# Shared read-outs and kept keys, and three sums of squares moved to ScalarE, in a hybrid attention, SSD and mLSTM block

## The chip, the cores and the metric

The kernel runs on one core of one Trainium2 chip. The metric is the device time of one execution, in microseconds (us), and lower is better. The engines are named as in the profile: PE (TensorE matmul) with PEld (its weight load), DVE (VectorE), ACT (ScalarE), POOL (GpSimd) and SP (the queue that issues most DMAs).

## The reference

Two token sequences (256 and 1024 tokens, width 1024) run through the same two layers, all in float32. Cut to what matters here:

```python
h = rmsnorm(x); [aq ak av | sz sxbc sdt | mq mk mv mo mi mf] = h @ W_in
x = x + concat(attention, bidirectional_ssd, bidirectional_mlstm) @ W_out
x = x + expert_choice_swiglu_moe(rmsnorm(x))

# mLSTM, per head (4 heads of 64), in chunks of 128, forward and backward
c_loc = einsum('bhcs,bcshe,bcshd->bched', w, vc, kc)     # state of a chunk: weighted keys times values
wq    = exp(dmat - m_l) * (q @ k.T)                      # inside the chunk, masked
num   = wq @ v + einsum(q, c_prev, sc)                   # + read-out of the state before the chunk
den   = max(|sum(wq) + einsum(q, n_prev, sc)|, exp(-m_l))
h     = rmsnorm(h_f + h_b) per head; y = sigmoid(o) * h
# SSD, per chunk: y = (cb * exp(segsum)) @ xdt + C @ prev * exp(a_cs)
# attention: q = rmsnorm(aq), k = rmsnorm(ak), per head
```

## The kernel before

Both sequences stand side by side as T = 1280 tokens, that is NC = 10 chunks of P = 128. Each engine has its own instruction stream, written out by hand, that runs in order and waits on semaphores. `link` makes an engine wait for its own last result before its next instruction. Float32 matmuls show two records each in the profile (transposes one). A layer has these stages, in this order of time:

- The input projection is cut into "units". A unit is 8 matmuls that accumulate over the model width (16 records); between units PE does the small products of the mixers, so that the mixers run in the shade of the projection. ACT copies each unit out of PSUM (`evac`).
- **SSD loop**, 10 chunks. Per chunk PE does 3 units, `ssd_products` and `ssd_sum`. The latter ends with four matmuls of 64 rows and 256 columns (two directions by two groups) that read the state before the chunk, `PREV`.
- **State loop of the mLSTM**, 8 steps (`STEPS`; the forward and the backward scan take one chunk each per step). PE: `turn_keys(n+1)` (4 transposes of the keys of two chunks into PSUM), one unit, and the state product. DVE: `weigh_keys(n+1)` multiplies the turned keys by their weights (from PSUM) and then updates the state. ACT only copies the unit out.
- **mLSTM loop**, 10 chunks, which is where most of the change lies. SP loads a row table for chunk c into one of two buffers `DMM[c % 2]` (`m_load`, which waits until chunk c-2 has been summed by PE, `nd_made`). The streams, in their own order, are, for c = 0 to 9:
  - PE: unit c, `ml_products(c+1)`, `ml_sum(c)`. The latter has 8 matmuls of 65 columns from `DMM` and `V`, and then 8 of 64 rows and 65 columns with the states `PREVM`. It waits for `ml_weights(c)` and for `ml_read(c-1)`.
  - POOL: `ml_mask(c+1, 0)`, `ml_mask(c+1, 1)` (L713); from c = 1, wait for `h_summed` of chunk c-1 and take the reciprocal root of its four sums (`rroot`, L643 and L644); for c = 2, 4, 6, 8 `attn_root` (the same on the six sums of q and k of an attention chunk); for c = 3, 5 `attn_norm` (L724, L728).
  - ACT: `ml_exp(c+1, 0)` (4 exponentials of 128 columns, L1001, after mask (c+1, 0)), wait for `ml_gate(c-2)`, `Tanh` of the output gate (L1010), `evac` of unit c (L890), `ml_exp(c+1, 1)`.
  - DVE: `ml_read(c-1)` (two operations of 520 columns out of PSUM), `ml_gate(c-2)` (after the root), `ml_output(c-1)` (the last three operations of which are the sum of the two directions, its square and the sum of squares per head, L1427), `attn_product` (q and k squared, odd c) or `attn_sum` (L1441, even c, from 2), and `ml_weights(c+1)` (two operations, after the exponentials).
- Output projection with the attention between its parts, then the experts, which are half of the span and are not touched.

Of the kernel before, what the change touches and what calls it, by code (L numbers as in the profile page):

```python
# [8 lines left out]
P = 128  # L9
NC = T // P  # L10
NP = SEQS[0] // P
KD = D // P
HD = 64
# [66 lines left out]
def has_next(i):  # L80
    return i not in (NP - 1, NC - 1)


STEPS = [i for i in range(NC) if has_next(i)]


# [42 lines left out]
def program(nc, wi, wo, wga, wup, wdn, par, cst, onehot, xp, xs_in, yp, ys, btab, h2p, h2s, flip):  # L129
# [4 lines left out]
    with ctx:  # L134
# [43 lines left out]
        UROW = VO[0:4, 0:2 * T].rearrange("p (d t) -> p d t", d=2)  # L178
        MROW = VO[0:4, 2 * T:4 * T].rearrange("p (d t) -> p d t", d=2)
        PREVM = MID[:, pv_at:pv_at + 2 * NC * 130].rearrange("p (d c h e) -> p d c h e", d=2, c=NC, h=2)  # L180
        QT = HT[:, 6144:6144 + 2 * T].rearrange("p (j t) -> p j t", j=2)
# [38 lines left out]
        JUNK = HT[:, 5 * D:6 * D]  # L220
        SQ = TMP[:, 1104:1488]

        AFF = [TMP[:, 0:512], SCR[:, 3584:4096]]
# [78 lines left out]
        layer_cleared = sem("layer_cleared")  # L302
        table_stored = sem("table_stored")
        bias_loaded = sem("bias_loaded")
# [7 lines left out]
        def layer_sem(name):  # L312
# [35 lines left out]
        mrow_stored = layer_sem("mrow_stored")  # L348
        cs_loaded = [layer_sem(f"cs_loaded{j}") for j in range(2)]
        m_loaded = [layer_sem(f"m_loaded{j}") for j in range(2)]  # L350
        d_shifted = layer_sem("d_shifted")
# [71 lines left out]
        w_made = layer_sem("w_made")  # L423
        kt_turned = layer_sem("kt_turned")
        mstate_made = layer_sem("mstate_made")
        wk_made = layer_sem("wk_made")
# [21 lines left out]
        quad_spread = layer_sem("quad_spread")  # L448
        kept_sems = [cst_loaded, hot_loaded, layer_done, layer_cleared, table_stored, bias_loaded, *x_loaded, *gathered, *quad_gathered, scattered_p,
                     scattered_s]  # L450
# [40 lines left out]
        with nc.Block(no_gpsimd_drain=True) as block:  # L491
            @block.sync
            def _(sp):
                for layer in range(DEPTH):
# [75 lines left out]
                    def cs_load(c):  # L570
                        if c >= 2:
                            sp.wait_ge(y_made, c - 1)
                        sp.dma_start(DM[:, c % 2],
                                     bass.AP(tensor=csr.tensor, offset=c * 24 * P, ap=[[0, P], [12 * P, 2], [1, 8 * P]])).then_inc(cs_loaded[c % 2], 16)

                    def m_load(c):
                        if c >= 2:
                            sp.wait_ge(nd_made, c - 1)
                        sp.dma_start(DMM[:, c % 2].rearrange("p d h t -> p (d h t)"),
                                     bass.AP(tensor=mrr.tensor, offset=c * 8 * P, ap=[[0, P], [1, 8 * P]])).then_inc(m_loaded[c % 2], 16)  # L580

                    sp.wait_ge(csrow_stored, 16)
                    sp.wait_ge(state_made, len(STEPS))
                    for c in range(NC):
                        cs_load(c)
                        if layer == 0 and c == 1:
                            sp.wait_ge(state_kept, len(STEPS))
                            sp.dma_start(btab[:, 0:NREL], table).then_inc(table_stored, 16)
                        if layer == 0 and c == 4:
                            sp.wait_ge(table_stored, 16)  # L590
# [45 lines left out]
            def _(pool):  # L636
                for layer in range(DEPTH):
# [34 lines left out]
                    def ssd_mask(c, d):  # L672
                        if d == 0:
                            pool.wait_ge(cs_loaded[c % 2], 16 * (c // 2 + 1))
# [33 lines left out]
                    def ml_mask(c, d):  # L708
                        if d == 0:
                            pool.wait_ge(m_loaded[c % 2], 16 * (c // 2 + 1))  # L710
# [132 lines left out]
            def _(act):  # L843
                for layer in range(DEPTH):
# [148 lines left out]
                    evac(U_ATT - 1)  # L993

                    for i in range(NC):
                        evac(U_ATT + i)
                    def ml_exp(c, d):
                        act.wait_ge(md_masked, 2 * c + d + 1)
                        for h in range(MH):
                            v = DMM[:, c % 2, d, h, :]  # L1000
                            link(act.activation(v, v, ACT.Exp, bias=U[:, c, d, h:h + 1], scale=-1.0), md_exp if h == MH - 1 else act_chain)  # L1001

                    ml_exp(0, 0)
                    ml_exp(0, 1)
                    for c in range(NC):
# [6 lines left out]
                        if c + 1 < NC:  # L1012
                            ml_exp(c + 1, 1)

                    def attn_exps(n, h0=0, h1=AH):
# [146 lines left out]
            def _(dve):  # L1162
                for layer in range(DEPTH):
# [212 lines left out]
                    def weigh_keys(n):  # L1376
                        dve.wait_ge(kt_turned, n + 1)
                        if n >= 2:
                            dve.wait_ge(mstate_made, n - 1)
                        for d in range(2):  # L1380
                            c = scan_chunk(d, STEPS[n])
                            tt(heads(WK[n % 2][:, 256 * d:256 * d + 256], 4), heads(ps[:, 4 + 2 * (n % 2), 256 * d:256 * d + 256], 4),
                               wide(WM[:, c, d, :], HD), ALU.mult, wk_made)
# [21 lines left out]
                    nd = TMP[:, 0:520]  # L1405
                    hsd = SCR[:, 3392:3904]
                    hs, hd = hsd[:, 0:256], hsd[:, 256:512]
# [10 lines left out]
                    def ml_output(c):  # L1418
# [4 lines left out]
                        link(dve.reciprocal(rec, den))  # L1423
                        tt(heads(hsd, 8), heads(nd, 8)[:, :, 0:HD], wide(rec, HD), ALU.mult)
                        tt(hs, hs, hd, ALU.add)
                        tt(hd, hs, hs, ALU.mult)
# [61 lines left out]
                    for c in range(NC):  # L1488
# [7 lines left out]
                        if c >= 1:  # L1496
                            ml_output(c - 1)
                        if 1 <= c <= 8:
                            if c % 2:
                                attn_product(c // 2)  # L1500
                            else:
                                attn_sum(c // 2 - 1)
                        if c + 1 < NC:
# [216 lines left out]
            def _(pe):  # L1720
                for layer in range(DEPTH):
# [177 lines left out]
                    def ssd_sum(c):  # L1899
# [26 lines left out]

                    def turn_keys(n):
                        if n >= 2:
                            pe.wait_ge(wk_made, 2 * (n - 1))
                        for d in range(2):  # L1930
                            c = scan_chunk(d, STEPS[n])
                            for q in range(2):
                                last = pe.transpose(ps[:, 4 + 2 * (n % 2), 256 * d + q * P:256 * d + (q + 1) * P],  # L1933
                                                    QK[:, 2 + q, c * P:(c + 1) * P], ident)
                        last.then_inc(kt_turned, 1)
# [33 lines left out]
                    def ml_sum(c):  # L1969
# [6 lines left out]
                        for j in range(2):  # L1976
                            for d in range(2):
# [468 lines left out]
```

## Time and profile before

| | |
|---|---|
| median of 3 runs | 2414.69 us (2413.03 to 2416.08) |
| profiled execution | 2412.42 us, span 2411.0 us |
| granted TensorE clock, mean | 0.991 |
| PE busy | 2336.8 us, 97% of the span |
| DVE busy | 1046.9 us, 43% |
| ACT busy | 585.4 us, 24% |
| POOL busy | 538.1 us, 22% |

The busy times are those of one profiled execution, in which the span runs from the first instruction to the last; 1.4 us of that execution lie around it. PE's busy time is modelled at its ends and hides short waits, so the starts of its instructions say more than its share.

### The profile page before, as it was taken

Reading aid. Unit: us, or ns where it says so; the run is one execution under the profiler, and the core shown is the slowest. Engines: PE = TensorE matmul, PEld = TensorE weight load, DVE = VectorE, ACT = ScalarE, POOL = GpSimd, SP = SyncE. Lnnn points to the kernel's source line nnn. Section 1 sums busy time; section 2 is a strip of 40 time slices with the busy share of each in tenths; the row PEclk is TensorE's granted clock in tenths of the full one; section 3 lists DMA queues with packets and bytes.
Section 4 is the critical chain, followed back from the end, with each engine's and each line's share of the span. In section 5 each row is a group of like instructions: output and inputs, shape, how many; then the busy total and the mean of one; then the engine's idle time right before and its main releaser. Section 6 shows DMA issues by size and latency. Waiting matters only on the chain.

```text
span 2411.0 us, 34301 instructions
## 1 busy us (share of the span) xinstructions
PE 2336.8 (97%) x13630; PEld 1683.5 (70%) x13630; DVE 1046.9 (43%) x1961; ACT 585.4 (24%) x1265; POOL 538.1 (22%) x550
## 2 busy tenths in 40 slices
PE   7999999999999999999889999999999999999998
PEld 4577578874555788877645775788745468888786
DVE  4851566596645111111148515665965451111111
ACT  3220232344332111111132202323443321111111
POOL 1011453144211111111110114531442111111111
PEclk9999999999999999999999999999999999999999
DMA  3102222121227988778331012221212279887783
GB/s 131 38 18 70 71 90 81 62 97 53 79 76 268 327 289 280 265 262 287 92 121 38 18 65 76 80 78 62 97 54 79 79 270 329 286 281 258 269 287 79
DMA packets 149344, 352.24 MB, mean 146 GB/s; under 512 B 9885, under 2 KB 38049, under 8 KB 149186
## 3 DMA queue, kind: packets, MB, share of 16 engines
q1 hardware_dynamic: 134210, 308.11, 35.5%
q0 software_dynamic: 14976, 41.95, 7.0%
q8 instruction: 109, 1.79, 0.3%
q14 instruction: 49, 0.40, 0.1%
HBM read 307.75 MB, written 42.28 MB: 145 GB/s over the span
## 4 chain that ended last, share of the span: by engine, by line
PE 86%; DVE 7%; DMA 2%; ACT 2%; issue 1%; POOL 1%; SPq 1%; DVEq 0%; POOLq 0%; ACTq 0%; PEldq 0%
PE ps L1724 81%; DVE SCR L1168 2%; PE ps L2268 1%; PE ps L2015 1%; ACT SCR L1001 1%; DVE MID L1294 1%; DVE TMP L1168 1%; PE ps L2078 1%; DMA SCR<-cs_rows 1%; PE ps L1740 1%; DVE SCR L1177 1%; DMA SCR<-m_rows 0%; DVE HT L1168 0%; DMA HT<-h_sample,idxs 0%; PE ps L1933 0%
## 5 line engine op out<-in xcount | busy, mean ns | idle before, releaser
L1724 PE MATMUL ps<-MID,HT 128*128 128x512 f32 (+2 forms) x2240 | 608.4, 500 | 2.9 <-PE ps L1724 2.9
L1724 PE MATMUL ps<-HT,MID 128*128 128x160 f32 (+2 forms) x4192 | 575.4, 304 | 5.2 <-DVE HT L1168 5.2
L1724 PEld LDWEIGHTS ps<-HT,MID 128*128 128x128 f32 (+1 forms) x4192 | 560.4, 190 | 25.2 <-issue 23.9
L1724 PE MATMUL ps<-RING,HT 128*128 128x256 f32 (+2 forms) x2080 | 466.7, 391 | 2.5 <-DVE RING L1172 1.3
L1724 PEld LDWEIGHTS ps<-RING,HT 128*128 128x128 f32 (+1 forms) x2080 | 372.8, 190 | 85.9 <-issue 37.1
L1724 PEld LDWEIGHTS ps<-MID,HT 128*128 128x128 f32 (+1 forms) x2240 | 231.4, 151 | 227.3 <-issue 206.0
L1724 PE MATMUL ps<-HT,RING 128*128 128x512 f32 (+1 forms) x960 | 353.6, 526 | 0.0
L1177 DVE SCALAR_TENSOR_TENSOR HT<-HT,ps 128x160 f32<-128x160 f32 (+1 forms) x128 | 40.8, 319 | 683.2 <-ACT HT L1132 658.6
L1724 PEld LDWEIGHTS ps<-HT,RING 128*128 128x128 f32 x960 | 181.3, 192 | 160.7 <-issue 153.1
L824 POOL DMA_INDIRECT y_prompt<-SCR,idxp x32 | 50.5, 1578 | 618.4 <-ACT SCR L1142 617.8
L1132 ACT ACTIVATE HT<-ps 128x160 f32<-128x160 f32 (+1 forms) x128 | 38.6, 302 | 520.4 <-PE ps L1724 512.4
L1168 DVE TENSOR_TENSOR HT<-ps,part 128x512 f32<-128x512 f32 (+1 forms) x172 | 109.3, 635 | 70.2 <-PE ps L1740 22.5
L668 POOL TENSOR_TENSOR SCR<-MID,small 128x512 f32<-128x512 f32 x32 | 40.2, 1256 | 328.2 <-ACT MID L902 263.4
L1168 DVE TENSOR_TENSOR SCR<-SCR,ps 128x512 f32<-128x512 f32 x80 | 55.0, 687 | 134.3 <-POOL SCR L682 108.3
L1724 PE MATMUL ps<-MID 128*64 128x128 f32 (+3 forms) x1136 | 97.5, 304 | 4.1 <-DVE SCR L1168 2.9
L1138 ACT ACTIVATE SCR<-ps,small 128x512 f32<-128x512 f32 x64 | 44.0, 687 | 215.4 <-PE ps L1724 215.4
L1724 PEld LDWEIGHTS ps<-MID 64*128 64x128 f32 (+1 forms) x1136 | 73.1, 170 | 28.6 <-issue 17.1
L1168 DVE TENSOR_TENSOR SCR<-SCR,small 128x1024 f32<-128x1024 f32 (+1 forms) x60 | 74.8, 1247 | 35.4 <-POOL SCR L677 33.4
L737 POOL TENSOR_TENSOR SCR<-SCR,small 128x1536 f32<-128x1536 f32 (+1 forms) x20 | 48.7, 2436 | 160.8 <-DVE small L1475 160.8
L1168 DVE TENSOR_TENSOR TMP<-MID,small 128x256 f32<-128x256 f32 (+1 forms) x64 | 27.0, 422 | 132.0 <-PE ps L1724 130.9
L1724 PE MATMUL ps<-MID,SCR 128*128 128x65 f32 (+1 forms) x640 | 79.5, 278 | 4.2 <-DVE TMP L1168 4.2
L1724 PEld LDWEIGHTS ps<-MID,SCR 128*128 128x128 f32 x640 | 74.8, 192 | 9.1 <-issue 6.0
(239 smaller groups left out, 2130.3 us busy)
## 6 DMA issues: line engine op xcount, KB each, us to landing
MID<-w_gate SPq DMA_DIRECT2D x32, 2048.0 KB
MID<-w_up SPq DMA_DIRECT2D x32, 2048.0 KB
MID<-w_down SPq DMA_DIRECT2D x32, 2048.0 KB
RING<-w_in SPq DMA_DIRECT2D x22, 1024.0 KB, 5.3
SCR<-cs_rows SPq DMA_DIRECT2D x20, 1024.0 KB, 5.2
SCR<-m_rows SPq DMA_DIRECT2D x20, 512.0 KB, 3.8
MID<-w_out SPq DMA_DIRECT2D x8, 1024.0 KB, 6.7
y_sample<-RING SPq DMA_DIRECT2D x16, 512.0 KB, 2.6
```

What stands on the lines that cost most here:

```text
L668: link(pool.tensor_tensor(DXS[:, n % 2, d, :].rearrange("p (h e) -> p h e", h=SH), XS[:, c, :].rearrange("p (h e) -> p h e", h=SH), WS[:, ...
L737: link(pool.tensor_tensor(v, v, ADEN[n % 2].unsqueeze(2).to_broadcast([P, AH, nk * P]), ALU.mult), pn_made)
L824: pool.indirect_dma_start(yp4, bass.IndirectOffsetOnAxis(ap=idxp[:, e:e + 1], axis=0), YOP[e % 2], None, compute_op=ALU.add, bounds_check= ...
L1001: link(act.activation(v, v, ACT.Exp, bias=U[:, c, d, h:h + 1], scale=-1.0), md_exp if h == MH - 1 else act_chain)
L1132: link(act.activation(THG[:, 0:cols], ps[:, 2 + f % 2, 0:cols], ACT.Tanh, scale=0.5), gate_tanh)
L1138: link(act.mul(YO[e % 2][:, hf * 512:(hf + 1) * 512], ps[:, 4 + hf, :], gts[:, e:e + 1]), down_scaled)
L1168: link(dve.tensor_tensor(out, a, b, op), to)
L1177: link(dve.scalar_tensor_tensor(out=out, in0=a, scalar=x, in1=b, op0=op0, op1=op1), to)
L1294: link(dve.tensor_tensor_scan(m, u, u, MPREV[:, d, c:c + 1], ALU.max, ALU.max))
L1724: return pe.matmul(out, a, b, start=start, stop=stop)
L1740: last = pe.transpose(ps[:, 4 + 2 * (c % 2) + j, k * P:(k + 1) * P], XN[c][:, (4 * j + k) * P:(4 * j + k + 1) * P], ident)
L2015: last = pe.transpose(ps[:, 6 + h % 2, b * P:(b + 1) * P], PSC[n % 2][:, h, b * P:(b + 1) * P], ident)
```

## The change

It has four parts, in both layers.

1. SSD loop: the four read-outs of `PREV` become two, of 512 columns each (both directions in one matmul). mLSTM loop: the eight read-outs of `PREVM` become four, of 130 columns.
2. State loop: keys are turned once per pair of chunks (5 times, not 8), ACT copies them from PSUM to SBUF (`keep_keys`, 5 copies of 512 columns), and `weigh_keys` reads the copy.
3. mLSTM loop, chunks 0 to 8: the squares and the sums of squares of the heads are made by ACT (`head_squares`, four `Square` activations of 64 columns with a row sum), after `ml_exp(c+1, 1)` in its stream, and raise `h_summed`. The last chunk is still done by DVE.
4. The squares of q and k of the first four attention chunks are made by ACT, before `head_squares`, for c = 1, 3, 5, 7. Their sums stay on DVE.

Some semaphores are merged (`cs_loaded` and `m_loaded` into `rows_loaded`, `table_stored` into `hot_loaded`), with the same waits.

```diff
+KEY_PAIRS = []                    # (0,1) (2,9) (3,8) (4,7) (5,6)
+for _i in STEPS:
+    _pair = (scan_chunk(0, _i), scan_chunk(1, _i))
+    if not any(set(_pair) == set(x) for x in KEY_PAIRS):
+        KEY_PAIRS.append(_pair)
+def pair_of(n):
+    c = scan_chunk(0, STEPS[n])
+    return next(i for i, x in enumerate(KEY_PAIRS) if c in x)
...
+                    def keep_keys(i):
+                        act.wait_ge(kt_turned, i + 1)
+                        link(act.copy(KEYS[:, 2 * i:2 * i + 2, :], ps[:, 4 + 2 * (i % 2), :].rearrange("p (c n) -> p c n", c=2)), keys_kept)
+
+                    keep_keys(0)
                     for i in range(NC):
                         evac(U_ATT + i)
+                        if i + 1 < len(KEY_PAIRS):
+                            keep_keys(i + 1)
...
+                    def attn_product(n):
+                        if n >= 1:
+                            act.wait_ge(a_squared, n)
+                        link(act.activation(SQ, Z[:, ORDER[n], 0:384], ACT.Square), sq_made)
+
+                    def head_squares(c):
+                        act.wait_ge(h_ready, c + 1)
+                        for h in range(MH):
+                            at = slice(HD * h, HD * (h + 1))
+                            link(act.activation(HSD[:, 256:512][:, at], HSD[:, 0:256][:, at], ACT.Square, accum_out=ssb[:, h:h + 1]),
+                                 h_summed if h == MH - 1 else act_chain)
...
                         if c + 1 < NC:
                             ml_exp(c + 1, 1)
+                        if c in (1, 3, 5, 7):
+                            attn_product(c // 2)
+                        if c >= 1:
+                            head_squares(c - 1)
...
                     def weigh_keys(n):
-                        dve.wait_ge(kt_turned, n + 1)
+                        i = pair_of(n)
+                        dve.wait_ge(keys_kept, i + 1)
...
-                            tt(..., heads(ps[:, 4 + 2 * (n % 2), 256 * d:256 * d + 256], 4), ...)
+                            tt(..., heads(KEYS[:, 2 * i + KEY_PAIRS[i].index(c), :], 4), ...)
...
                         tt(heads(hsd, 8), heads(nd, 8)[:, :, 0:HD], wide(rec, HD), ALU.mult)
+                        if c < NC - 1:
+                            tt(hs, hs, hd, ALU.add, h_ready)
+                            return
...
-                        if 1 <= c <= 8:
-                            if c % 2:
-                                attn_product(c // 2)
-                            else:
-                                attn_sum(c // 2 - 1)
+                        if c in (2, 4, 6, 8):
+                            dve.wait_ge(sq_made, c // 2)
+                            attn_sum(c // 2 - 1)
...
-                        for d in range(2):
-                            for g in range(2):
-                                last = mm(ps[:, 6 + g, 256 * d:256 * d + 256], BC[64 * g:64 * g + 64, 1, t:t + P],
-                                          PREV[64 * g:64 * g + 64, d, c, :])
+                        for g in range(2):
+                            last = mm(ps[:, 6 + g, :].rearrange("p (d n) -> p d n", d=2), BC[64 * g:64 * g + 64, 1, t:t + P],
+                                      PREV[64 * g:64 * g + 64, :, c, :])
...
-                    def turn_keys(n):
-                        if n >= 2:
-                            pe.wait_ge(wk_made, 2 * (n - 1))
+                    def turn_keys(i):
+                        if i >= 2:
+                            pe.wait_ge(keys_kept, i - 1)
...
-                        if n + 1 < len(STEPS):
+                        if n + 1 < len(KEY_PAIRS):
                             turn_keys(n + 1)
...
-                            for d in range(2):
-                                for q in range(2):
-                                    b = 64 * q
-                                    last = mm(ps[:, 4 + 3 * q, 65 * (2 * d + j):65 * (2 * d + j) + 65],
-                                              QK[b:b + 64, j, c * P:(c + 1) * P], PREVM[b:b + 64, d, c, j, :])
+                            for q in range(2):
+                                b = 64 * q
+                                out = ps[:, 4 + 3 * q, 0:260].rearrange("p (d j e) -> p d j e", d=2, j=2)[:, :, j, :]
+                                last = mm(out, QK[b:b + 64, j, c * P:(c + 1) * P], PREVM[b:b + 64, :, c, j, :])
```

## Rows read from the trace of the kernel before

**Rows 1.** Windows: the mLSTM loop, layers 1 and 2; PE, PEld, DVE, ACT, POOL, clock, DMA.

```profile
453.46:530.38 76.92, 74.62 (x561) 64.63 (x559) 63.49 (x125) 39.73 (x100) 29.48 (x44) 0.98 0.24 83
1658.37:1734.56 76.19, 73.12 (x562) 63.41 (x560) 63.20 (x125) 39.73 (x100) 28.88 (x44) 1.00 0.25 84
```

**Rows 2.** Waits in the first loop; total us, times, longest us.

```profile
ACT SCR L1001 <- POOL SCR L713: 28.7, 8, 5.4
```

**Rows 3.** Timeline of PE, one chunk: start us, us, instructions.

```profile
500.03 3.72 PE L1724 MATMUL ps<-RING,HT 128*128 128x256 f32 x16
503.68 0.72 PE L1724 MATMUL ps<-MID 64*128 64x128 f32 x8
504.33 2.00 PE L1724 MATMUL ps<-MID,SCR 128*128 128x65 f32 x16
506.25 1.11 PE L1724 MATMUL ps<-MID 64*128 64x65 f32 x16
507.29 3.72 PE L1724 MATMUL ps<-RING,HT 128*128 128x256 f32 x16
```

**Rows 4.** Timeline of DVE in the same stretch.

```profile
500.19 0.56 DVE L1168 TENSOR_TENSOR TMP<-MID 128x384 f32<-128x384 f32 x1
...
507.97 0.42 DVE L1427 TENSOR_REDUCE small<-SCR 128x4 f32<-128x256 f32 x1
...
509.01 1.41 DVE L1168 TENSOR_TENSOR SCR<-SCR,ps 128x512 f32<-128x512 f32 x2
510.46 0.70 DVE L1168 TENSOR_TENSOR TMP<-ps,small 128x520 f32<-128x520 f32 x1
```

**Rows 5.** Timeline of POOL in the first loop.

```profile
465.56 1.54 POOL L713 TENSOR_SCALAR_AFFINE_SELECT SCR<-SCR 128x512 f32<-128x512 f32 x2 [47.37 <-DMA SCR<-m_rows]
...
501.97 0.62 POOL L724 TENSOR_TENSOR RING<-MID,SCR 128x256 f32<-128x256 f32 x1
502.67 0.40 POOL L728 TENSOR_TENSOR RING<-MID,SCR 128x128 f32<-128x128 f32 x1
504.23 1.60 POOL L713 TENSOR_SCALAR_AFFINE_SELECT SCR<-SCR 128x512 f32<-128x512 f32 x2 [1.17 <-DMA SCR<-m_rows]
508.55 0.19 POOL L643 TENSOR_SCALAR small<-small 128x4 f32<-128x4 f32 x1 [2.72 <-DVE small L1427]
...
509.92 0.20 POOL L643 TENSOR_SCALAR SCR<-SCR 128x6 f32<-128x6 f32 x1
...
511.67 1.41 POOL L713 TENSOR_SCALAR_AFFINE_SELECT SCR<-SCR 128x512 f32<-128x512 f32 x2
```

**Rows 6.** Timeline of ACT in the same stretch.

```profile
505.15 1.70 ACT L1001 ACTIVATE SCR<-SCR,small 128x128 f32<-128x128 f32 x4 [3.30 <-POOL SCR L713]
...
507.74 1.70 ACT L1001 ACTIVATE SCR<-SCR,small 128x128 f32<-128x128 f32 x4
512.40 1.71 ACT L1001 ACTIVATE SCR<-SCR,small 128x128 f32<-128x128 f32 x4 [2.96 <-POOL SCR L713]
```

**Rows 7.** Timeline of ACT in the router: an exponential with a row sum.

```profile
582.99 0.31 ACT L1047 ACTIVATE MID<-MID,small 128x16 f32<-128x16 f32 x1 [4.93 <-DVE MID L1172]
583.21 0.19 ACT L1047 ACTIVATION_READ_ACCUMULATOR MID<-MID,small 128x1 f32 x1
```

**Rows 8.** Instruction groups of ACT over the whole span (busy us, mean ns | idle).

```profile
L916 ACT ACT_TABLE_LOAD x2 | 2.6, 1283 | 0.0
```

**Rows 9.** Timeline of PE in the state loop.

```profile
439.40 0.69 PE L1724 MATMUL ps<-MID,TMP 128*64 128x65 f32 x16
...
444.06 0.69 PE L1724 MATMUL ps<-MID,TMP 128*64 128x65 f32 x16
...
448.33 0.69 PE L1724 MATMUL ps<-MID,TMP 128*64 128x65 f32 x16
```

**Rows 10.** Timeline of PE in the SSD loop: the inter-chunk read-outs.

```profile
316.06 1.14 PE L1724 MATMUL ps<-MID 64*128 64x256 f32 x8
```

**Rows 11.** Timeline of PE after the mLSTM loop.

```profile
535.15 1.14 PE L1724 MATMUL ps<-RING,HT 64*128 64x256 f32 x8
```

More of the change, by code:

```diff
@@ L179, in program @@
         MROW = VO[0:4, 2 * T:4 * T].rearrange("p (d t) -> p d t", d=2)
+        KEYS = MID[:, bc_at:bc_at + 2 * NC * P].rearrange("p (c n) -> p c n", c=NC)
         PREVM = MID[:, pv_at:pv_at + 2 * NC * 130].rearrange("p (d c h e) -> p d c h e", d=2, c=NC, h=2)
@@ L221, in program @@
         SQ = TMP[:, 1104:1488]
+        HSD = SCR[:, 3392:3904]
         AFF = [TMP[:, 0:512], SCR[:, 3584:4096]]
@@ L302, in program @@
         layer_cleared = sem("layer_cleared")
-        table_stored = sem("table_stored")
         bias_loaded = sem("bias_loaded")
@@ L348, in program @@
         mrow_stored = layer_sem("mrow_stored")
-        cs_loaded = [layer_sem(f"cs_loaded{j}") for j in range(2)]
-        m_loaded = [layer_sem(f"m_loaded{j}") for j in range(2)]
+        rows_loaded = [layer_sem(f"rows_loaded{j}") for j in range(2)]
+        h_ready = layer_sem("h_ready")
+        sq_made = layer_sem("sq_made")
         d_shifted = layer_sem("d_shifted")
@@ L424, in program @@
         kt_turned = layer_sem("kt_turned")
+        keys_kept = layer_sem("keys_kept")
         mstate_made = layer_sem("mstate_made")
@@ L448, in program @@
         quad_spread = layer_sem("quad_spread")
-        kept_sems = [cst_loaded, hot_loaded, layer_done, layer_cleared, table_stored, bias_loaded, *x_loaded, *gathered, *quad_gathered, scattered_p,
+        kept_sems = [cst_loaded, hot_loaded, layer_done, layer_cleared, bias_loaded, *x_loaded, *gathered, *quad_gathered, scattered_p,
                      scattered_s]
@@ L573, in cs_load @@
                         sp.dma_start(DM[:, c % 2],
-                                     bass.AP(tensor=csr.tensor, offset=c * 24 * P, ap=[[0, P], [12 * P, 2], [1, 8 * P]])).then_inc(cs_loaded[c % 2], 16)
+                                     bass.AP(tensor=csr.tensor, offset=c * 24 * P, ap=[[0, P], [12 * P, 2], [1, 8 * P]])).then_inc(rows_loaded[c % 2], 16)
                     def m_load(c):
@@ L579, in m_load @@
                         sp.dma_start(DMM[:, c % 2].rearrange("p d h t -> p (d h t)"),
-                                     bass.AP(tensor=mrr.tensor, offset=c * 8 * P, ap=[[0, P], [1, 8 * P]])).then_inc(m_loaded[c % 2], 16)
+                                     bass.AP(tensor=mrr.tensor, offset=c * 8 * P, ap=[[0, P], [1, 8 * P]])).then_inc(rows_loaded[c % 2], 16)
                     sp.wait_ge(csrow_stored, 16)
@@ L587, in _ @@
                             sp.wait_ge(state_kept, len(STEPS))
-                            sp.dma_start(btab[:, 0:NREL], table).then_inc(table_stored, 16)
+                            sp.dma_start(btab[:, 0:NREL], table).then_inc(hot_loaded, 16)
                         if layer == 0 and c == 4:
-                            sp.wait_ge(table_stored, 16)
+                            sp.wait_ge(hot_loaded, 32)
                             sp.dma_start(bia, bass.AP(tensor=btab.tensor, offset=0, ap=[[1, P], [512, AH], [1, 384]])).then_inc(bias_loaded, 16)
@@ L673, in ssd_mask @@
                         if d == 0:
-                            pool.wait_ge(cs_loaded[c % 2], 16 * (c // 2 + 1))
+                            pool.wait_ge(rows_loaded[c % 2], 16 * (c // 2 + 1))
                         v = DM[:, c % 2, d, :].rearrange("p (h t) -> p h t", h=SH)
@@ L709, in ml_mask @@
                         if d == 0:
-                            pool.wait_ge(m_loaded[c % 2], 16 * (c // 2 + 1))
+                            pool.wait_ge(rows_loaded[c % 2], 16 * (NC // 2 + c // 2 + 1))
                         v = DMM[:, c % 2, d]
@@ L1381, in weigh_keys @@
                             c = scan_chunk(d, STEPS[n])
-                            tt(heads(WK[n % 2][:, 256 * d:256 * d + 256], 4), heads(ps[:, 4 + 2 * (n % 2), 256 * d:256 * d + 256], 4),
+                            tt(heads(WK[n % 2][:, 256 * d:256 * d + 256], 4), heads(KEYS[:, 2 * i + KEY_PAIRS[i].index(c), :], 4),
                                wide(WM[:, c, d, :], HD), ALU.mult, wk_made)
@@ L1405, in _ @@
                     nd = TMP[:, 0:520]
-                    hsd = SCR[:, 3392:3904]
+                    hsd = HSD
                     hs, hd = hsd[:, 0:256], hsd[:, 256:512]
@@ L1925, in _ @@
                     pe.wait_ge(y_gated, NC)
-                    def turn_keys(n):
-                        if n >= 2:
-                            pe.wait_ge(wk_made, 2 * (n - 1))
-                        for d in range(2):
-                            c = scan_chunk(d, STEPS[n])
+                    def turn_keys(i):
+                        if i >= 2:
+                            pe.wait_ge(keys_kept, i - 1)
+                        for d, c in enumerate(KEY_PAIRS[i]):
                             for q in range(2):
-                                last = pe.transpose(ps[:, 4 + 2 * (n % 2), 256 * d + q * P:256 * d + (q + 1) * P],
+                                last = pe.transpose(ps[:, 4 + 2 * (i % 2), 256 * d + q * P:256 * d + (q + 1) * P],
                                                     QK[:, 2 + q, c * P:(c + 1) * P], ident)
@@ L1976, in ml_sum @@
                         for j in range(2):
-                            for d in range(2):
-                                for q in range(2):
-                                    b = 64 * q
-                                    last = mm(ps[:, 4 + 3 * q, 65 * (2 * d + j):65 * (2 * d + j) + 65],
-                                              QK[b:b + 64, j, c * P:(c + 1) * P], PREVM[b:b + 64, d, c, j, :])
+                            for q in range(2):
+                                b = 64 * q
+                                out = ps[:, 4 + 3 * q, 0:260].rearrange("p (d j e) -> p d j e", d=2, j=2)[:, :, j, :]
+                                last = mm(out, QK[b:b + 64, j, c * P:(c + 1) * P], PREVM[b:b + 64, :, c, j, :])
                         last.then_inc(nd_made, 1)
```

## The prediction

> **What bounds the kernel now.** I read the page first: PE is busy for 97% of the span and is most of the chain that ended last, so a change pays where it takes time from PE, and costs where it makes PE wait. Then the windows of the stages that the change touches, and then the timelines of each engine there, because the share of PE hides waits. SSD loop and state loop: PE runs without gaps, the others wait for it. mLSTM loop: 76.92 and 76.19 us in the two layers, and DVE is busy for 63 of them [rows 1]. PE's own work for a chunk is 7.26 us: unit 3.65, products 0.65, first half of the sum 1.92, read-outs 1.04 [rows 3]. Ten of these are 72.6, so some 4 us a layer are waits: DVE works without a gap through most of the loop, and a chunk takes 7.3 to 7.7. ACT is busy for only 40 of the 77 [rows 1], which makes it look free. But the order of its stream matters more than its load: it waits 28.7 us for POOL's masks [rows 2], and POOL's stream has the root between two masks.
>
> **mLSTM loop, what is removed.** DVE loses the square of the heads and the sum, about 0.45 each (0.42 busy for the sum [rows 4]; the square has half the work of an operation of 512 columns), and, every second chunk, 0.59 for the square of q and k [rows 4]. PE loses half of its 64-row read-outs. They took 1.04 for 16 records of 65 columns; 8 records of 130 columns are, in shape, the products (8 of 128 columns, 0.65) [rows 3], so I take 0.65, a gain of 0.39 a chunk where PE sets the pace. The bounds are 0 and 0.52.
>
> **mLSTM loop, what is added: a ring.** Before, `h_summed` came from DVE, which had it ready without ACT. Now the sums of chunk c-1 are made by ACT *after* `ml_exp(c+1, 1)`. POOL waits for them before its root, and only then, in its own order, comes to `ml_mask(c+2, 0)`; ACT's next exponentials wait for that mask. So one chunk's period can't be shorter than this chain, once around:
>
> - mask start to first exponential: 0.73 (511.67 to 512.40) [rows 5, 6]
> - four exponentials, tanh, copy of the unit, four exponentials: 4.29 (505.15 to 509.44) [rows 6]
> - four squares with a row sum. The trace before has none of this shape. The nearest is an exponential of 16 columns with a sum, 0.41 from its start to the end of the read of the accumulator [rows 7]; 64 columns cost a little more, an immediate scale a little less. I take 0.40 each, 1.60; bounds 0.30 (the sum's read hidden) and 0.50.
> - from the last sum to POOL's start: 0.16 (508.39 to 508.55) [rows 4, 5]
> - POOL's root: 1.37 (508.55 to 509.92) [rows 5]
>
> That is 8.15, already above the 7.26 to 7.7 of now. On top of it, in the same two streams: for even c `attn_root`, 1.75 (509.92 to 511.67) [rows 5]; for c = 3 and 5 `attn_norm`, 1.10 and a step, 1.18 [rows 5]; for odd c the square of q and k on ACT, 384 columns, three times a 128-column exponential's columns, 0.56. The waits inside the ring are covered: the heads' sum (`h_ready`) is ready about 3.3 after POOL's root, which is what a chunk of 7.7 leaves for gate and output without weights (1.45), read (1.46), q and k (0.6) and the two removed (0.9) [rows 1, 4], and ACT comes to it 5.0 after the root at the earliest. The copy of `m_rows`, 4.2 after the sum that frees the buffer (500.03 to 504.23) [rows 3, 5], is done before POOL is.
>
> The schedule, from the start of unit 0. The first mask that waits starts at 12.10 now [rows 1, 5] (465.56 less 453.46), and 0.39 earlier then, 11.70, as PE's first sum is shorter. The periods from mask to mask are then 8.71 (c = 1), 9.90, 9.89, 9.90, 9.89, 9.90, and 8.71 (c = 7): the last mask, of chunk 9, starts at 78.6. Exponentials done 5.02 later, 83.6; last weights 0.75, 84.4; DVE's read of chunk 8, which is queued behind these weights, 1.46 [rows 4], 85.9; PE's last sum, 1.92 + 0.65, ends at 88.5. Against 76.92 and 76.19 that is +11.6 and +12.3, together **+23.9**. The gain of PE is lost in it: PE waits about 3 us a chunk.
>
> POOL's operations stretch when DVE works in SBUF: the two masks took 1.60 once and 1.41 another time [rows 5]. DVE's gate and output now fall beside `attn_root` and the mask. I add 0.2 a period (0 to 0.4), 14 periods: **+2.8**. After the loop, the first scores came 4.8 after its end [rows 1, 11]; DVE is now late there with a gate, the copies for the attention, an output and a read, so I add 0.7 a layer (0 to 1.5): **+1.4**.
>
> **State loop.** A step with key transposes takes 4.66, one without 4.27 [rows 9]. PE has no gap in either, so each of the 3 removed is worth 0.39, six in all: **-2.3**. The five copies, some 0.6 each, go to ACT, which only copies one unit a step (0.4); the first weighing comes about 1 us later, and PE's first state product is a unit away. Cover gone, they would cost 0.6 each. Reading keys from SBUF: no change on DVE's free time.
>
> **SSD loop.** Two 512-column read-outs for four of 256: the same columns. 8 records of 64 rows and 256 columns are 1.14 busy [rows 10], 8 of 128 columns 0.72 [rows 3]: 1024 more columns cost 0.42, so 4 of 512 come out at 0.72 - 0.42 + 0.84 = 1.14 too. **0**. If the two row groups overlap less in the longer pieces, half of a 512-column piece (0.21) a chunk is lost, +4.3 in all; a gain of 0.1 a chunk, -2, is the other end.
>
> **Sum.** 23.9 + 2.8 + 1.4 - 2.3 = +25.8: the profiled execution, 2412.4, would be at 2438, and as the median of the runs is 2.3 above it, I say **2440 us**.
>
> **A rule that speaks against the change.** The page "ScalarE: Activation LUTs" of the Trainium skill says, under "Rules for kernel authors", to give multiplications and additions to VectorE. It gives a reason by element; the ring above does not rest on it. The same page (What ACT_TABLE_LOAD costs) prices an ACTIVATE with immediates at 186 ns and 0.833 ns a column, 0.24 us for 64 columns as an estimate, with no price for the sum; by it alone, without the read of the accumulator that the trace shows [rows 7], the squares would be 0.64 a period cheaper, and the time 9 us less, 2431.
>
> **The rivals.**
>
> - *PE sets the pace* (0.05): the end on the other side. What speaks for it: DVE is the late engine now, and is relieved by 0.9 to 1.5 a chunk. Then a chunk is 6.87, the loop some 69.5 with its first wait and last transposes, -14.1, and with the state loop -16.4: 2398. It needs a ring of at most 6.87, but the ring without the squares is 6.55, so four squares would have to take 0.3. From a ring of about 7.6 on it is slower.
> - *Table loads* (0.01): were `Square` in another table than `Exp`, each chunk would pay two loads of 1.28 [rows 8], 18 a layer: +46, 2487. Against it: the SSD loop already has a `Square` among exponentials in each chunk, and no load lies in that loop.
> - *A flat ring* (0.05): `attn_root`, `attn_norm` and the squares of q and k cost nothing, 8.15 a period. The last mask is then at 68.8 and the loop at 78.7, +4.3, in all +6 with the terms above, 2421; with cheap squares it is no change. The written order speaks against it: they stand between the root and the mask.
> - *No change* for another reason (0.03).
>
> **How the numbers follow.** The ring has 0.86. Its own range: squares 0.30 or 0.50 move it by 56 x 0.1 = 5.6; contention by 2.8; the SSD loop by -2 or +4.3; the tail by -1.4 or +1.6. Taken all one way it is 2428 to 2454; I take 2430 to 2452 for 8 in 10, which leaves the rivals out. 0.2% (5 us) is about what a measurement of this kernel can tell from no change. Faster: 0.05. Same: the no-change case and half of the flat ring, 0.06. Slower: 0.89.
>
> **What would show it.** In the mLSTM loop, units that start 9.5 to 10 us apart from c = 3 on, with about 8.7 at the ends; PE waits for DVE; ACT's exponentials wait for POOL's L713, POOL's L643 for ACT's `Square`, and the mask follows `attn_root` or `attn_norm` at once, with no wait for `m_rows`. DVE waits before the gate. State loop: the three last turned steps at 4.27. SSD loop: unchanged. It is wrong if POOL's root does not wait for ACT, or if a square with its sum is far from 0.40.

## The result

The kernel after takes **2443.03 us** (median of 4 runs, 2438.55 to 2447.31) against 2413.86 of the kernel before on the same chip: a ratio of 1.0131, with a 95% interval of 1.0117 to 1.0145. By the medians that is 29.2 us slower (2443.03 / 2413.86 is 1.0121, inside the interval); forecast were 2440 in a range of 2430 to 2452. The profiled execution of the kernel after took 2444.55 us (span 2443.1), that of the kernel before 2412.42, so 32.1 us are to be found between the two traces.

The windows of the two mLSTM loops, from the first record of unit 0 to the end of the last read-outs, in the kernel after; columns as in [rows 1]:

```profile
454.01:546.93 92.92, 80.73 (x482) 67.23 (x480) 54.87 (x104) 52.98 (x168) 29.77 (x44) 0.87 0.21 69
1674.70:1765.25 90.55, 79.95 (x481) 67.38 (x479) 54.23 (x101) 52.97 (x168) 29.77 (x44) 0.88 0.21 70
```

Beside [rows 1] the loops are 16.00 and 14.36 us longer: 30.4 of the 32.1. DVE lost 9 us of work a loop and ACT gained 13, yet neither is busy for more than 60% of the loop, and PE is busy for 87 to 88% at a lower clock. No engine has become the bound by its load. What has, the waits of the first loop say (total, times, longest):

```profile
POOL small L659 <- ACT SCR L1037: 44.5, 8, 5.8
ACT SCR L1024 <- POOL SCR L729: 30.4, 8, 4.9
DVE SCR L1209 <- ACT SCR L1024: 27.9, 16, 4.6
PEld ps L1767 <- DVE SCR L1209: 9.4, 8, 2.8
```

POOL's root waits for ACT's squares (L1037), and ACT's exponentials (L1024) wait for POOL's mask (L729), eight times each: the two engines wait for each other. DVE and PE come behind. Two turns of the ring, first the timeline of POOL:

```profile
484.44 1.77 POOL L729 TENSOR_SCALAR_AFFINE_SELECT SCR<-SCR 128x512 f32<-128x512 f32 x2
492.05 0.19 POOL L659 TENSOR_SCALAR small<-small 128x4 f32<-128x4 f32 x1 [5.84 <-ACT SCR L1037]
492.32 1.01 POOL L660 TENSOR_TENSOR small<-small 128x4 f32<-128x4 f32 x1
493.41 0.61 POOL L740 TENSOR_TENSOR RING<-MID,SCR 128x256 f32<-128x256 f32 x1
...
494.71 1.42 POOL L729 TENSOR_SCALAR_AFFINE_SELECT SCR<-SCR 128x512 f32<-128x512 f32 x2
501.42 0.19 POOL L659 TENSOR_SCALAR small<-small 128x4 f32<-128x4 f32 x1 [5.29 <-ACT SCR L1037]
...
503.08 1.35 POOL L660 TENSOR_TENSOR SCR<-SCR,small 128x6 f32<-128x6 f32 x1
504.58 1.77 POOL L729 TENSOR_SCALAR_AFFINE_SELECT SCR<-SCR 128x512 f32<-128x512 f32 x2
```

The same of ACT:

```profile
485.53 1.70 ACT L1024 ACTIVATE SCR<-SCR,small 128x128 f32<-128x128 f32 x4 [4.42 <-POOL SCR L729]
...
488.11 1.70 ACT L1024 ACTIVATE SCR<-SCR,small 128x128 f32<-128x128 f32 x4
489.85 0.52 ACT L1030 ACTIVATE TMP<-MID 128x384 f32<-128x384 f32 x1
490.40 0.26 ACT L1037 ACTIVATE SCR<-SCR 128x64 f32<-128x64 f32 x1
490.56 0.19 ACT L1037 ACTIVATION_READ_ACCUMULATOR SCR<-SCR 128x1 f32 x1
490.78 0.26 ACT L1037 ACTIVATE SCR<-SCR 128x64 f32<-128x64 f32 x1
```

Read it in turn: a mask starts at 484.44, exponentials from 485.53 to 489.81, square of q and k, four squares, root at 492.05, norm, and at 494.71 the next mask, with no wait for `m_rows` ahead of it (the loop has one such wait, of 45.6 us, and it ends with the first mask that waits, at 465.61). From there it goes round again, with the q and k root (503.08) in the place of the norm: the mask after it starts at 504.58. The eight masks of the first loop that wait start at 465.61, 474.32, 484.44, 494.71, 504.58, 514.86, 524.74 and 533.78: periods of 8.71, 10.12, 10.27, 9.87, 10.28, 9.88 and 9.04. From the first to the last are 68.17 us, in either layer.

PE in the last third of the first loop:

```profile
530.96 0.71 PE L1767 MATMUL ps<-MID 64*128 64x128 f32 x8 [2.40 <-DVE SCR L1209]
532.52 3.65 PE L1767 MATMUL ps<-MID,SCR 128*128 128x65 f32 x16 [0.84 <-DVE TMP L1209]
536.09 1.24 PE L1767 MATMUL ps<-MID 64*128 64x130 f32 x8
537.26 6.09 PE L1767 MATMUL ps<-RING,HT 128*128 128x256 f32 x16
...
544.45 1.90 PE L1767 MATMUL ps<-MID,SCR 128*128 128x65 f32 x16
546.28 0.72 PE L1767 MATMUL ps<-MID 64*128 64x130 f32 x8
```

And windows of 5 us there (columns as in [rows 1]):

```profile
525.00:530.00 5.00, 3.56 (x16) 2.79 (x16) 1.66 (x3) 3.89 (x10) 1.37 (x2) 1.00 0.34 105
530.00:535.00 5.00, 3.20 (x20) 3.04 (x21) 3.28 (x6) 2.28 (x11) 2.28 (x4) 0.69 0.00 0
535.00:540.00 5.00, 5.00 (x21) 4.11 (x21) 4.01 (x9) 4.62 (x16) 0.44 (x1) 0.50 0.01 2
```

PE waits 2.40 us ahead of the products and 0.84 ahead of the sum. Then its granted clock is 0.50, which is 1.2 GHz: the same 16 records of the sum take 3.65 instead of 1.90, the same unit 6.09 instead of the 3.72 of [rows 3].

Outside the loops, PE's timeline in the state loop and at the read-outs of the SSD loop and of the mLSTM loop, to be held against [rows 9], [rows 10] and [rows 3]:

```profile
431.81 0.69 PE L1767 MATMUL ps<-MID,TMP 128*64 128x65 f32 x16
436.07 0.69 PE L1767 MATMUL ps<-MID,TMP 128*64 128x65 f32 x16
...
388.20 1.13 PE L1767 MATMUL ps<-MID 64*128 64x512 f32 x4
...
460.57 0.72 PE L1767 MATMUL ps<-MID 64*128 64x130 f32 x8
461.21 3.72 PE L1767 MATMUL ps<-RING,HT 128*128 128x256 f32 x16
```

### The profile page after: what moved, and what is told of

Same layout as the page of the kernel before. It is cut to its first block, busy times and chain, and to the rows that moved or that the text cites. A ratio compares the mean times of both kernels' runs of the same rounds, so it can differ in the third digit from the quotient of the medians.

```text
span 2443.1 us, 33925 instructions
## 1 busy us (share of the span) xinstructions
PE 2351.5 (96%) x13366; PEld 1679.5 (69%) x13366; DVE 1028.6 (42%) x1917; ACT 620.9 (25%) x1427; POOL 540.6 (22%) x550
## 4 chain that ended last, share of the span: by engine, by line
PE 84%; ACT 5%; DVE 4%; POOL 2%; DMA 2%; issue 1%; SPq 1%; POOLq 0%; DVEq 0%; ACTq 0%; PEldq 0%
PE ps L1767 79%; ACT SCR L1024 2%; PE ps L2308 1%; PE ps L2055 1%; DVE MID L1335 1%; ACT SCR L1037 1%; PE ps L2118 1%; DMA SCR<-cs_rows 1%; PE ps L1783 1%; POOL small L660 1%; DVE SCR L1209 1%; POOL SCR L729 1%; DVE SCR L1218 1%; DMA HT<-h_sample,idxs 0%; DVE HT L1209 0%
## 5 line engine op out<-in xcount | busy, mean ns | idle before, releaser
L1767 PE MATMUL ps<-RING,HT 128*128 128x256 f32 (+2 forms) x2080 | 477.7, 397 | 2.5 <-DVE RING L1213 1.3
L1767 PEld LDWEIGHTS ps<-RING,HT 128*128 128x128 f32 (+1 forms) x2080 | 379.4, 194 | 97.8 <-issue 44.8
L1767 PE MATMUL ps<-MID 128*64 128x128 f32 (+3 forms) x896 | 92.6, 333 | 15.8 <-DVE SCR L1209 14.6
L1209 DVE TENSOR_TENSOR TMP<-MID,small 128x256 f32<-128x256 f32 (+1 forms) x96 | 40.7, 424 | 134.9 <-PE ps L1767 127.2
L1767 PE MATMUL ps<-MID,SCR 128*128 128x65 f32 (+1 forms) x640 | 85.3, 290 | 10.1 <-DVE TMP L1209 9.9
L1767 PEld LDWEIGHTS ps<-MID,SCR 128*128 128x128 f32 x640 | 80.4, 204 | 15.3 <-issue 12.6
L1767 PEld LDWEIGHTS ps<-MID 64*128 64x128 f32 (+1 forms) x896 | 58.3, 171 | 40.1 <-DVE SCR L1209 20.4
```

The costliest lines, as they stand in the source:

```text
L1209: link(dve.tensor_tensor(out, a, b, op), to)
L1767: return pe.matmul(out, a, b, start=start, stop=stop)
```

## The experiments

The theory: the ring over ACT and POOL sets the period, closed by the placing of the heads' sums on ACT. Rivals after the result: that PE's lower clock is the cause, and not an effect; that ACT's added work as such, or one of the other parts, costs the time. In each edit "-" is a line of the kernel after. "Loop" is, for both layers, the time from the start of the first products to the end of the last read-outs: 93.57 and 91.19 in the kernel after, 77.57 and 76.84 before. "Masks" are the periods from the start of one waiting pair of masks to the next. Each ratio is to runs of the kernel before in the same round; their median was 2410.62 in experiments 1, 2, 4 and 5, 2412.16 in 3, 7 and 8, and 2412.2 in 6 and 9. Where no number of runs is given, it is 4 or 5.

**1. The sums of the heads back on DVE, all other parts kept.**

```diff
                         if c in (1, 3, 5, 7):
                             attn_product(c // 2)
-                        if c >= 1:
-                            head_squares(c - 1)
...
-                        if c < NC - 1:
-                            tt(hs, hs, hd, ALU.add, h_ready)
-                            return
                         tt(hs, hs, hd, ALU.add)
```

> The changed kernel with the squares and sums of the heads back on DVE; shared read-outs, kept keys and the squares of q and k on ACT stay. Ring theory (POOL's root waits for ACT's sums, ACT's next exponentials for the mask behind the root): the ring is open, chunks start 7.1 to 7.5 us apart, the loop takes some 73 us a layer, and the kernel is a little faster than before, about 2407 us. Rival, the shared read-outs or the kept keys cost the time: 2435 or more. Rival, ACT's load costs it: in between.

Measured: 2406.4 us (10 runs), 0.9982 [0.9972, 0.9992] of before. The whole loss is gone; loops 75.09 and 75.69, where 73 was expected. First the window of the first loop in this kernel, then the starts of `ml_weights` (DVE multiplies a chunk's exponentials by its products of q and k, in two operations) for three chunks:

```profile
452.71:527.16 74.45, 71.02 (x481) 60.04 (x480) 60.86 (x118) 41.80 (x104) 28.30 (x44) 0.98 0.25 86
```

```profile
483.67 1.41 DVE L1207 TENSOR_TENSOR SCR<-SCR,ps 128x512 f32<-128x512 f32 x2
...
491.46 1.41 DVE L1207 TENSOR_TENSOR SCR<-SCR,ps 128x512 f32<-128x512 f32 x2
...
498.60 1.41 DVE L1207 TENSOR_TENSOR SCR<-SCR,ps 128x512 f32<-128x512 f32 x2
```

A chunk takes 7.79 and 7.14, DVE works through between them without a gap, and the clock is back at 0.98 (0.95 in the second layer). So DVE sets the pace again in these chunks, as before, and PE's 6.87 a chunk is not reached.

**2. The heads' sums alone moved; read-outs, keys and the squares of q and k as before.** The edit takes the code of the kernel before for these three parts.

> Only the squares and sums of the heads on ACT; read-outs, key transposes and the squares of q and k as before. Ring theory: masks 8.3 apart with no q and k work, 10.1 with the root of q and k, 9.6 with the norm; some +27 us against before, about 2441. Rival, read-outs or keys: no change, 2414 to 2418.

Measured: 2438.58, 1.0116 [1.0099, 1.0133]; loops 89.37 and 89.39. The masks are 8.16 and 8.49 apart at the ends, 10.12, 9.87 and 9.87 with the root of q and k, and 9.72 and 9.74 with the norm, as expected within 0.25. This one part makes nearly the whole loss.

**3. Read-outs and keys alone.** The edit of 1, and the squares of q and k back on DVE as well.

> Shared read-outs and kept keys alone, all squares on DVE as before. Key transposes -2.3 us; the shorter read-outs give little, since DVE sets the pace in most chunks (7.5 apart): -2 us; about 2410, against 2414 before. If PE set the pace: 0.39 a chunk, -8 more, 2404.

Measured: 2409.45 (12 runs), 0.9991 [0.9982, 0.9999]; loops 75.73 and 77.98. A small gain at most.

**4. The root and the norm of q and k behind the next masks in POOL's stream.** The same work, outside the ring.

```diff
                             ml_mask(c + 1, 1)
+                        if c - 1 in (2, 4, 6, 8):
+                            attn_root((c - 1) // 2 - 1)
+                        if c - 1 in (3, 5):
+                            attn_norm((c - 1) // 2 - 1)
...
                             rroot(rsb, ssb, MH, 4.0 / HD, 4 * EPS, h_rooted)
-                        if c in (2, 4, 6, 8):
-                            attn_root(c // 2 - 1)
-                        if c in (3, 5):
-                            attn_norm(c // 2 - 1)
```

> The changed kernel with POOL's root and norm of q and k moved behind the next two masks in its stream; same instructions. Ring theory: 1.75 and 1.18 us leave the ring, masks are 8.2 (even chunks) and 8.7 (odd) apart in place of 10, -15 us against the changed kernel, about 2428. Rival, ACT's load or TensorE's clock by itself sets the pace: no change, 2443.

Measured: 2425.85, 1.006 [1.004, 1.0079]; loops 83.24 and 83.70. POOL's timeline there:

```profile
484.98 1.66 POOL L729 TENSOR_SCALAR_AFFINE_SELECT SCR<-SCR 128x512 f32<-128x512 f32 x2
...
487.01 1.32 POOL L660 TENSOR_TENSOR SCR<-SCR,small 128x6 f32<-128x6 f32 x1
492.47 0.19 POOL L659 TENSOR_SCALAR small<-small 128x4 f32<-128x4 f32 x1 [4.13 <-ACT SCR L1037]
492.75 1.01 POOL L660 TENSOR_TENSOR small<-small 128x4 f32<-128x4 f32 x1
493.90 1.66 POOL L729 TENSOR_SCALAR_AFFINE_SELECT SCR<-SCR 128x512 f32<-128x512 f32 x2
```

The long root (487.01) now fills a part of POOL's wait instead of making it longer. The periods are 8.92 and 8.39, with and without ACT's square of q and k, where they were 10.27 and 9.88: the ring without what stood in it by order. From the first mask to the last are 60.64 and 60.63 us in place of 68.17, 15.1 less in both layers together, as forecast. The loops are 17.8 shorter; the rest comes after the last mask (10.30 and 10.65 us to the loop's end, against 13.15 and 10.72).

**5. The squares ahead of the second exponentials in ACT's stream.**

```diff
                         evac(U_ATT + NC + c)
+                        if c >= 1:
+                            head_squares(c - 1)
                         if c + 1 < NC:
                             ml_exp(c + 1, 1)
                         if c in (1, 3, 5, 7):
                             attn_product(c // 2)
-                        if c >= 1:
-                            head_squares(c - 1)
```

> The changed kernel with the head sums ahead of the second group of exponentials in ACT's stream; same instructions. Ring theory: POOL no longer waits for the second group (1.7 us); the ring closes through DVE's output instead, masks about 8.5 to 9 apart, -9 to -12 us against the changed kernel, about 2432. Rival, ACT's load or the clock by itself: no change, 2443.

Measured: 2424.4, 1.005 [1.0033, 1.0066], a larger gain than expected; loops 83.82 and 84.91. ACT's timeline there:

```profile
475.07 0.37 ACT L906 COPY MID<-ps 128x256 f32<-128x256 f32 x1
476.45 0.26 ACT L1037 ACTIVATE SCR<-SCR 128x64 f32<-128x64 f32 x1 [1.01 <-DVE SCR L1209]
...
477.97 1.70 ACT L1024 ACTIVATE SCR<-SCR,small 128x128 f32<-128x128 f32 x4
481.96 1.71 ACT L1024 ACTIVATE SCR<-SCR,small 128x128 f32<-128x128 f32 x4 [2.28 <-POOL SCR L729]
```

The mask waits for `m_rows` again at four of the seven later chunks (0.43 to 1.90 us), and the squares now wait for DVE: with the four exponentials (1.70) out of it, the ring is no longer alone in setting the period. The gain is in the masks, 59.39 and 60.07 us from the first to the last in place of 68.17, 16.9 in all, where the loops are 16.0 shorter. It isn't the clock: the last unit of the first layer took 3.72 here, but an earlier one took 5.76, and from the last mask to the loop's end it is 12.13 and 12.42 us, together no less than in the kernel after.

**6. Both orders, 4 and 5 together.**

> Both reorderings at once: head sums ahead of the second exponentials on ACT, and POOL's root and norm of q and k behind the next masks. If with the sums earlier DVE's output closes the loop: no faster than the sums earlier alone, 2424. If POOL's root of q and k is still in the ring there (masks were 9.2 to 9.4 apart after it, 7.9 to 8.8 after the others): 0.5 us less in three periods a layer and more, 2418 to 2421. Still slower than before in both.

Measured: 2421.04, 1.0039 [1.0025, 1.0053]; loops 84.56 and 84.50. The interval overlaps that of 5, so the difference between them is not clear of noise. The two gains don't add. In the first loop six later masks now wait for `m_rows`, by 0.65 to 2.40 us, a copy that starts after PE has summed the chunk that used the buffer: the mask has come to wait for another chain. What that chain is made of was not tried. With both orders mended the squares on ACT still cost more than they give.

**7. The clock as the cause.** Two more matmuls of a constant, whose results nobody uses, between unit and products from chunk 3 on, in PE's waiting time. PE also waits there until ACT has copied the unit out.

```diff
                         unit(U_ATT + NC + c)
+                        if 3 <= c < NC - 1:
+                            pe.wait_ge(proj_read, U_ATT + NC + c)
+                            keep_clock((U_ATT + NC + c + 1) % 2, 2)
```

> The changed kernel with two idle matmuls of 384 columns (1.3 us) ahead of the products of chunks 4 to 9, where PE waits 0.5 to 2.4 us, so that TensorE is less idle; their results are not used. If the low clock late in the loop costs time beside the ring: clock near 1.0 in the loop, last unit 3.7 us in place of 6.1, -4 to -6 us, about 2437. If the ring hides it: no change, 2443. If the clock is the whole cause: back to 2414. Masks stay 8.7 to 10.3 apart in all cases but the last.

Measured: 2439.59, 1.0118 [1.0102, 1.0134]. Window and PE's timeline of the first loop in this kernel:

```profile
451.68:541.68 90.00, 81.14 (x505) 65.78 (x504) 53.78 (x101) 52.98 (x168) 29.71 (x44) 0.96 0.20 71
```

```profile
530.13 1.97 PE L1767 MATMUL ps<-MID,SCR 128*128 128x65 f32 x16 [0.84 <-DVE TMP L1209]
...
532.68 3.72 PE L1767 MATMUL ps<-RING,HT 128*128 128x256 f32 x16
```

The clock went from 0.87 to 0.96 and the last unit from 6.09 to 3.72; the window of the loop got 2.9 shorter in this layer, while the masks kept their periods (8.70, 10.12, 10.27, 9.86). In the second layer the clock was 0.96 too, but the window was 91.81 against 90.55: the first mask came 0.4 later, and the last sum ran at the low clock here (2.83 us). Over the whole kernel the medians differ by 3.4 us, and the intervals of 1.0118 and 1.0131 overlap, so what the low clock costs in all is not measured. What is shown is that it is not what holds the chunks apart: 0.09 more clock left every mask period where it was.

**8. The order of 4 with the sums on DVE (1 and 4 together).**

> Head sums on DVE, and POOL's root and norm of q and k behind the next two masks. The masks then wait for the copy of m_rows alone; chunks 7.0 to 7.5 apart; about 1 us less than with the head sums on DVE alone, 2406. If POOL's order matters only while the ring is closed: the same as there, 2407.

Measured: 2407.83 (12 runs), 0.9976 [0.9964, 0.9989]; loops 74.93 and 75.36. The interval overlaps that of 1. The place of root and norm is worth some 17 us where the ring is closed (1.0131 less 1.006 of 2412; 15.1 of it in the mask periods), and nothing that was measured where it is open.

**9. Each square with its sum made twice**, the second writing the same values again.

> The changed kernel with each of the four squares with a row sum made twice (same inputs, same output), so the cost of the moved work is doubled. Ring theory: 1.52 us more in each of seven mask-to-mask periods, and once more at the last chunk's tail at most: masks 10.2 to 11.8 apart, +21 to +24 us against the changed kernel, about 2465. Rival, ACT has room (it is busy for 53 of 92 us in the loop) and the loss comes from elsewhere: under +5 us.

Measured: 2465.34, 1.0226 [1.0205, 1.0246]; loops 103.30 and 103.42. POOL's timeline there:

```profile
483.64 1.78 POOL L729 TENSOR_SCALAR_AFFINE_SELECT SCR<-SCR 128x512 f32<-128x512 f32 x2
492.78 0.19 POOL L659 TENSOR_SCALAR small<-small 128x4 f32<-128x4 f32 x1 [7.36 <-ACT SCR L1038]
...
495.44 1.42 POOL L729 TENSOR_SCALAR_AFFINE_SELECT SCR<-SCR 128x512 f32<-128x512 f32 x2
```

The period is 11.80 where it was 10.27, and POOL's wait 7.36 where it was 5.84: all four added squares, 4 x 0.38 = 1.52, are in it. Over the seven periods 10.6 us came on, 7 x 1.52. Nothing hides a square.

## Why the prediction was right

- **The ring's place.** As predicted, L659 waits for ACT's `Square`, the exponentials for L729, and no mask for `m_rows` from the second on. Experiment 1 opens the ring and the loss is gone; 9 lengthens it and the whole of the added time arrives; 4 takes the steps out that stood in it by order, and a period falls from 9.9-10.3 to 8.4-8.9. That is shown, not argued. It isn't ACT's load as such: 4 and 5 leave all of its work and get some 17 and 19 us back by order alone. What the 9 us are made of that are left with both orders (6) stays open. The flat ring (8.15 a period) is refuted by the periods of about 10; experiment 4 comes near it, with 8.39, and 8.92 where the square of q and k is still inside.
- **The ring's terms.** The turn from 484.44 to 494.71, against the terms predicted: mask to first exponential 1.09 (0.73), exponentials to the last one's end 4.32 with the gap behind it (4.29), square of q and k 0.55 (0.56), four squares 1.49 (1.60), to POOL 0.16 (0.16), heads' root and norm up to the mask 2.66 (1.37 + 1.18 = 2.55); together 10.27. So what I called contention is for the greater part one place: the pair of masks takes 1.77 at every second chunk instead of 1.42, and ACT's start waits for the first of them (0.36 of the 0.38 by which this turn is over the 9.89). The seven periods of the first layer are 68.17 us, forecast 66.9 and 1.4 of contention: 68.3. Two sizes were off and partly cancel: mask to exponential was too cheap by up to 0.36, and the square, 0.38 from start to start and not 0.40, was 0.1 a turn too dear, inside its bounds.
- **TensorE's clock, the term that was missing.** The last mask starts 79.77 and 79.83 after unit 0 (predicted 78.6 with 1.4 of contention, 80.0). From there to the loop's end I had 9.9; it took 13.15 and 10.72. That is 4.1 us too little, and the masks came 0.4 early; the difference, 3.7, is what the loops' +30.4 has over the predicted 23.9 + 2.8 = 26.7. DVE's last read ended 7.5 after the last mask in both layers (forecast 7.3), so the rest is PE's. Most of it is the first layer's last turn at 1.2 GHz, sums, read-outs and unit: units had started 9.3 to 10.2 apart from c = 3 on (forecast 9.5 to 10), but the last came 12.4 after the one before. In the second layer unit and sum ran at full clock and only the last read-outs did not (1.24 busy for 0.72). I had given PE 3 us of waiting a chunk and no price for what such waits do to its clock. The trace before had a hint of it that I overlooked: I read chunks of 7.3 to 7.7, but two of the first layer took 8.3 and 8.6 from unit to unit (475.91 to 484.21 to 492.77), and the unit at 484.21 took 5.01 where the others took 3.72. This 3.7, less 0.3 in the tail, is the 3.4 by which the medians' +29.2 is over the forecast +25.8. The range held because its room for other terms (the squares, the SSD loop) was not used; none of it was meant for the clock.
- **A closed price.** The Trainium skill, "ScalarE: Activation LUTs" (What ACT_TABLE_LOAD costs), gives 186 ns and 0.833 ns a column for an ACTIVATE with immediates, 0.24 us for 64 columns as an estimate. The trace has 0.26 for the ACTIVATE, near it; but the next one starts 0.38 later, behind a read of the accumulator of 0.19 that the formula leaves out, and by 9 it is this 0.38 that counts.
- **State loop, SSD read-outs, mLSTM read-outs.** State steps 4.27 apart (436.07 less 431.81), one turned pair fewer for each of three steps: -2.3, as predicted. The SSD read-outs take 1.13 instead of 1.14, and in both kernels the read-outs of chunks 3 to 6 start 14.0 apart: 0. The mLSTM read-outs take 0.64 (460.57 to 461.21): the predicted 0.39 gained, and lost again in the ring. Experiment 3 measures both together at -2.7 us, with an interval from -4.3 to -0.2.
- **Tail.** The first scores start 4.77 and 5.85 after the loops' ends, 1.1 more in all (predicted 1.4). That it came near is luck: the first layer has none of it, and the second layer's part is low clock (10 records of 512 columns take 5.23 where they took 4.46), not the late copies that I named.
- **The remainder.** The three terms, 30.4 + 1.1 - 2.3, make 29.2; the profiled pair differs by 32.1. The other 2.9 I can't lay to the change. 1.7 of it stands ahead of the first state loop: the first SSD read-outs come 3.2 later, and the SSD loop gives 1.4 back. Kernels with the same code up to there start unit 0 of the first mLSTM loop between 450.13 (experiment 9) and 456.22 (experiment 4), so I put this down to the spread of single executions; that was not tried further. It means, too, that the forecast of the profiled execution, 2438, was 6.5 us too low, while that of the median was 3.0 too low.
- **The squares of q and k** cost ring time too (0.55 at four chunks a layer, 4.4 in all): with the sums alone moved (2) the masks span 65.97 in each layer, 2.20 less than 68.17. With an open ring these squares on ACT give back some 1.5 us (the ratios 0.9982 and 0.9991 of 1 and 3 differ by 0.0009, 2 us, or by the medians' distances to before, 4.2 and 2.7, 1.5), which the intervals allow to be nothing.
- **The rival on the other side**, PE sets the pace, fell doubly: the ring wasn't under 6.87, and with the ring open (1) the chunks take 7.1 to 7.8 and not 6.87, since DVE's own work sets them. Its 2398 would not have come even with free squares; the best versions, 1 and 8, stand at 0.998.

## What to carry to other kernels

An engine that is busy for half of the time is not free: before work is moved to it, follow its stream in order. Start at the consumer of the moved work, go on through what that consumer does next, and see whether the chain comes back to a wait of the engine that now does the work; add up its parts. If the chain closes, its length is the least period, and everything that stands between in either stream by order alone is part of it, whatever its cause. Where the chain must be closed, first put what isn't part of it behind the instruction that others wait for (17 us here). Where it needn't be closed, leave it open: the small sum on the busiest engine was cheaper than the wait for it from the idle one.

## What the runs showed of the hardware

- TensorE's granted clock fell to 0.50 (1.2 GHz) in the loop after PE had waited ahead of products and sum (busy for 3.56 and 3.20 us of the 5 in the two windows shown), and a unit took 6.09 instead of 3.72. Two added matmuls a chunk brought the loop's mean clock from 0.87 to 0.96. The Trainium skill, "TensorE: Matmul & The Clock Gate" (Part 1), has the array at 1.2 or 2.4 GHz by how busy it has been; the windows at 0.50 and 1.00 agree with both levels. Units at the low clock stood in the middle of the loop too (4.97 us at 484.92, 5.30 at 514.97) and cost nothing that the masks show, whose periods stayed the same in experiment 7, where these two took 3.72; at the loop's end it cost some 3 us in the first layer and half of one in the second.
- Eight read-outs of 130 columns take 0.65 where sixteen of 65 took 1.04, but four of 512 take as long as eight of 256 (1.13 and 1.14).
- A row sum on ACT has a record of its own: 0.26 for the 64-column square, 0.19 for the read of the accumulator that begins before the first ends, and 0.38 from one square to the next, with four (490.40 to 490.78) as with eight in a row (experiment 9).
